# Hybrid layers: the four retention heads' features packed into three tiles, the forget logits moved into spare rows of a rotation tile

## The chip, the cores and the metric

The kernel runs on one core of one Trainium2 chip. The metric is the device time of one launch in microseconds (us); the kernel before was run three times, and the median of the three counts.

## The reference, cut to what matters

The whole program is two blocks of a network on 256 tokens with a model width of 1024, all in float32. The first block (two layers of feed-forward, recurrence and dilated attention) isn't touched by the change. The second block prepends 16 meta tokens (272 tokens in all) and runs two hybrid layers. A hybrid layer multiplies the tokens by one input matrix, splits the product into nine parts, mixes along the tokens in three ways, and multiplies the joined result by one output matrix:

```python
IN_SPLITS = (192, 192, 384, 384, 256, 384, 384, 384, 6)
def hybrid_layer(h, w_in, b_f, ret_gn_g, pool_w, pool_scale, w_out, ...):
    proj = jnp.einsum('bld,de->ble', h, w_in)
    q_r, k_r, v_r, g_r, u_p, q_f, k_f, v_f, f_logit = parts
    o_r = retention_chunkwise(rotary(q_r), rotary(k_r), v_r)
    o_r = silu(g_r) * head_group_norm(o_r, ret_gn_g)
    o_p = multiscale_pool(u_p, pool_w, pool_scale)
    logf = jax.nn.log_sigmoid(f_logit + b_f)
    o_f = forgetting_attention(q_f, k_f, v_f, logf)
    mix = jnp.concatenate([o_r, o_p, o_f], axis=-1)
    mix = jnp.einsum('ble,ed->bld', mix, w_out)
    h = layer_norm_2(ALPHA * h + mix, ln1_g, ln1_b)
```

Retention has 4 heads with 48 features in a query or key and 96 in a value, 384 value features together; `head_group_norm` normalises the 96 features of each head. Forgetting attention has 6 heads of 64 features and one forget logit per head and token. A feed-forward part follows each mixing part.

## The kernel before, in words

**Stages.** `plan()` writes the program as a list of stages, each a multiplication by one weight matrix. A stage is cut into chunks; a chunk holds the weights of one output tile of 128 features and is one DMA of 512 KB or more from SyncE (SP) into one of four slots `raw`. Float32 accuracy comes from a split: ScalarE (ACT) rounds a chunk to `whi` (L1068), VectorE (DVE) subtracts to get `wlo` (L1529), activations are split into `h_hi`/`h_lo` or `x_hi`/`x_lo` the same way, and TensorE (PE) forms three products per 128x128 block (`products`, L511 to L513). One output tile of a stage with K input tiles is thus 3K matmuls. Rounding runs two chunks ahead of PE (`round_ahead` on ACT, `rest_ahead` on DVE).

**A hybrid layer** is the stage `mix` (22 output tiles, K = 8) and the stage `mixo` (8 output tiles, K = `MIX_K` = 9). The order of everything is written out by hand: `MIX_ORDER` lists the output tiles of `mix`, and in `hybrid` of each engine a loop over the step s does the chunk's own work and then what stands under `if s == ...`. An engine's queue runs in program order and waits on semaphores.

The output tiles of `mix` are, in order: `gate 0`, the four rotation tiles `rot` (query halves, then key halves; each head takes 24 of 32 rows, 8 rows are spare), three `vr`, `k 0`, `q 0`, three `v`, `k 1`, `q 1`, `k 2`, `q 2`, two `pool`, and `gate 1` to `gate 3`. There are four gate tiles since each retention head has a tile of its own with 96 of 128 rows in use; rows 96 to 107 of `gate 0` hold the six forget logits twice.

**Around the front of `mix`:** ACT copies each product out of PSUM (`tile`, L1395); behind a norm it also forms `ax` in eight pieces (L1085, two at s = 1, three each at s = 2 and 3). `forget_logits` (ACT L1400 to L1402, with a load of the exp table) follows at s = 2, the copy `sel_r` (L1446) at s = 4. DVE runs `rotate(0)` (L1949 to L1951) at s = 3, the first part of the logarithm of the forget gate (`cumulative_logits(0)`, L1547 and L1548) at s = 4, `rotate(1)` at s = 5. PE runs `ret_scores` (L928) behind tile s = 6; it waits for all four rotations.

**Retention values.** `ret_values(h)` (L892) multiplies the decayed scores of head h by its values: three matmuls (112, 96 and 64 keys; 272, 160 and 64 token columns), 96 output rows, one PSUM bank per head, called for four heads behind tile 10. ACT copies and squares each head (L1438, L1439). `ret_variance` (L944) is four matmuls of 32 output columns each, one per head, side by side in the array. ACT takes the root (L1455), DVE the reciprocal (L2057). `ret_spread(h)` (L952) brings head h's factor to 96 rows, four times, each followed by DVE's `norm_output` (L2007); `gated` (L2015 to L2018) multiplies by the gate and splits, four times.

**Forgetting attention** works in pairs of heads: `fox_scores` (L864, L870), `fox_transposed` (L885), `fox_values` (L907; two heads, each 64 output columns wide, next to each other in the array and in one bank). `mixo` starts with seven of its nine K tiles on the first two chunks (`BEGIN_ORDER`), with `fox_values(2)` between them, and then runs chunk by chunk through `from_h`; DVE adds each output tile (L1645, L1659, L1668) and ACT squares it.

```python
            def ret_values(h):
                pe.wait_ge(vr_centred, l + 1)

                pe.wait_ge(ret_d, RET_HEADS * (l + 1))
                o = ps[0:RET_DV, out_bank[h], :]
                by_values(o, vr_tok, slice(RET_DV * h, RET_DV * (h + 1)), decayed(h)).then_inc(ret_o, 1)
```

Of the kernel before, what the change touches and what calls it, by code (L numbers as in the profile page):

```python
# [18 lines left out]
P = 128  # L19
# [28 lines left out]
RET_HEADS, RET_DK, RET_DV = 4, 48, 96  # L48
HALF_DK = RET_DK // 2
# [3 lines left out]
LOGIT_ROW = RET_DV  # L53
LOGIT_ROWS = 2 * FOX_HEADS
# [16 lines left out]
MIX_K = RET_HEADS + 2 + 3  # L71
MIX_ORDER = ([("gate", 0)] + [("rot", n) for n in range(4)] + [("vr", n) for n in range(3)] + [("k", 0), ("q", 0)]
             + [("v", n) for n in range(3)] + [("k", 1), ("q", 1), ("k", 2), ("q", 2), ("pool", 0), ("pool", 1)]
             + [("gate", n) for n in range(1, 4)])
# [13 lines left out]
C_PS = C_GN + LAYERS_2 * RET_HEADS  # L88
# [6 lines left out]
B_SEL = B_EXP + P  # L95
# [43 lines left out]
def build(nc, x_in, meta_in, par_in, con_in, bias_in, con2_in, poolw_in, weights, out):  # L139
# [34 lines left out]
    ident, ones_d, ones_head = con[:, 0:P], con[:, P:2 * P], con[:, 2 * P:3 * P]  # L174
# [44 lines left out]
    gsb = place("gsb", [RET_HEADS, TOK])  # L219
# [11 lines left out]
    osb = place("osb", [RET_HEADS, TOK])  # L231
# [28 lines left out]
    sqh = place("sqh", [RET_HEADS, TOK])  # L260
# [178 lines left out]
    carry = slice(LOGIT_ROW - HD, LOGIT_ROW - HD + LOGIT_ROWS)  # L439
# [67 lines left out]
    def _(pe):  # L507
# [316 lines left out]
        def hybrid(l):  # L824
# [15 lines left out]
            def fox_scores(pair):  # L840
# [3 lines left out]
                if pair == 0:  # L844
                    pe.wait_ge(c_done, l + 1)
                    pe.wait_ge(sel_done, l + 1)
                    pe.wait_ge(vr_centred, l + 1)

                    pe.wait_ge(ret_sq, RET_HEADS * l + 2)
# [39 lines left out]
            def by_values(o, v, col, weights_t):  # L889

                for k in range(3):
                    last = nc.tensor.matmul(o[:, QT_AT[k]:TOK], v[0:QT[k], k, col],  # L892
                                            weights_t[0:QT[k], KEY_AT[k]:KEY_AT[k] + KEY_COLS[k]], start=k == 0, stop=k == 2)
                return last

            def fox_values(pair):
                heads = (2 * pair, 2 * pair + 1)
                if pair == 0:

                    pe.wait_ge(ret_norm, RET_HEADS * (l + 1))  # L900
# [32 lines left out]
            def ret_values(h):  # L933
                pe.wait_ge(vr_centred, l + 1)

                pe.wait_ge(ret_d, RET_HEADS * (l + 1))
                o = ps[0:RET_DV, out_bank[h], :]
                by_values(o, vr_tok, slice(RET_DV * h, RET_DV * (h + 1)), decayed(h)).then_inc(ret_o, 1)

            def ret_variance():  # L940

                pe.wait_ge(ret_sq, RET_HEADS * (l + 1))
                for h in range(RET_HEADS):
                    ins = nc.tensor.matmul(ps[32 * h:32 * h + 32, 5, 0:TOK], ones_head[0:RET_DV, 0:32], sqh[0:RET_DV, h, :],  # L944
                                           start=True, stop=True, skip_group_check=True)
                ins.then_inc(ret_var, 1)

            def ret_spread(h):
                pe.wait_ge(ret_rstd, l + 1)
                if h:  # L950
                    pe.wait_ge(ret_norm, RET_HEADS * l + h)
                nc.tensor.matmul(ps[0:RET_DV, 5, 0:TOK], con2[32 * h:32 * h + 1, B_EXP:B_EXP + RET_DV],  # L952
                                 std4[32 * h:32 * h + 1, :], start=True, stop=True).then_inc(ret_bc, 1)
# [10 lines left out]
            for s in range(WIN_TILES):  # L964
                tile(s)
                if s == 6:
                    ret_scores()
                if s == 8:
                    pe.wait_ge(acc_free, mix_evicted(st, "vr", 2))
                    pe.wait_ge(ret_d, RET_HEADS * l + 1)  # L970
                    transposes(vr, 3, ((2, 0), (3, 0), (4, 0))).then_inc(vt2_done, 1)
                if s == 10:
                    for h in RET_ORDER:
                        ret_values(h)
                if s == 11:
                    fox_scores(0)
                if s == 12:
                    ret_variance()
                if s == 13:
                    pe.wait_ge(acc_free, mix_evicted(st, "v", 2))  # L980
                    pe.wait_ge(biased, f0 + 1)
                    transposes(vf, 3, ((2, 0), (3, 0), (4, 0))).then_inc(vt2_done, 1)
                if s == 14:
                    ret_spread(0)
                if s == 15:
# [3 lines left out]
                if s == 16:  # L989
                    fox_transposed(1)  # L990
                    ret_spread(2)
                if s == 17:
                    fox_scores(2)
                    ret_spread(3)
                if s == 18:
                    fox_values(0)
                    fox_transposed(2)
                if s == 19:
                    fox_transposed(3)
                if s == 20:  # L1000
                    fox_values(1)
                    fox_transposed(4)
                if s == 21:
# [5 lines left out]
            def ready(k):  # L1009

                if k < RET_HEADS:
                    pe.wait_ge(ret_ready, RET_HEADS * l + k + 1)
                elif k < RET_HEADS + 2:
                    pe.wait_ge(pool_ready, 2 * l + k - RET_HEADS + 1)
                else:
                    pe.wait_ge(at_ready, PAIRS + 3 * l + k - (RET_HEADS + 2) + 1)
# [37 lines left out]
    def _(act):  # L1054
# [314 lines left out]
        def hybrid(l):  # L1369
            st = by_name[f"mix{l}"]  # L1370
            f0 = FOX_HEADS * l
            lr = slice(LOGIT_ROW, LOGIT_ROW + LOGIT_ROWS)
# [24 lines left out]
            def forget_logits():  # L1397
                act.wait_ge(acc_free, mix_evicted(st, "gate", 0))
                bf = par[lr, C_BF + l:C_BF + l + 1]
                nc.scalar.activation(sgate[lr, 0, :], gsb[lr, 0, :], ACT.Identity, bias=bf).then_inc(fx_done, 1)  # L1400
                link(nc.scalar.activation(sgate[lr, 1, :], gsb[lr, 0, :], ACT.Abs, bias=bf))
# [21 lines left out]
            def round_output(hp):  # L1423
                act.wait_ge(pv_done, HEADS + f0 + 2 * hp + 2)
                nc.scalar.activation(h_hi[:, RET_HEADS + 2 + hp, :], acc(5, TOK), ACT.Copy).then_inc(at_hi, 1)
# [8 lines left out]
            hd = slice(0, RET_DV)  # L1434

            def copy_output(n, h):
                act.wait_ge(ret_o, RET_HEADS * l + n + 1)
                nc.scalar.activation(osb[hd, h, :], ps[hd, out_bank[h], 0:TOK], ACT.Copy).then_inc(ret_osb, 1)  # L1438
                nc.scalar.activation(sqh[hd, h, :], ps[hd, out_bank[h], 0:TOK], ACT.Square).then_inc(ret_sq, 1)  # L1439

            for s in range(WIN_TILES):
                round_ahead(st, s // SLOTS, s % SLOTS)
                if s == 2:
                    forget_logits()
                if s == 4:
                    nc.scalar.activation(sel_r[:, :], con2[:, B_SEL:B_SEL + FOX_HEADS * P], ACT.Copy).then_inc(sel_done, 1)  # L1446
                if s == 11:
                    for n, h in enumerate(RET_ORDER):
                        copy_output(n, h)
                if s == 12:  # L1450

                    nc.scalar.activation(spare[:, :], eps[:, :], ACT.Sqrt)
                if s == 13:
                    act.wait_ge(ret_var, l + 1)
                    nc.scalar.activation(std4[:, :], ps[:, 5, 0:TOK], ACT.Sqrt, bias=eps[:, 0:1]).then_inc(ret_std, 1)  # L1455
                    exps(0)
                if s == 14:
                    exps(1)
                    copy_values()
                if s == 16:  # L1460
                    copy_transposed(0)
                if s == 17:
                    copy_transposed(1)
                    exps(2)
                if s == 18:
                    exps(3)
                if s == 19:
# [3 lines left out]
                if s == 20:  # L1471
                    copy_transposed(3)
                    exps(5)
                if s == 21:
                    copy_transposed(4)
                    round_output(1)
                    act.wait_ge(acc_free, mix_evicted(st, "gate", 2))
                    nc.scalar.activation(gsb[:, 0:3, :], gsb[:, 0:3, :], ACT.Silu).then_inc(silu2, 1)
                tile(s)
            act.wait_ge(acc_free, mix_evicted(st, "gate", 3))  # L1480
            nc.scalar.activation(gsb[:, 3, :], gsb[:, 3, :], ACT.Silu).then_inc(silu2, 1)
            copy_transposed(5)
            act.wait_ge(pool_mm, l + 1)
            for m in range(2):
                nc.scalar.activation(h_hi[:, RET_HEADS + m, :], acc(2 + m, TOK), ACT.Copy,
# [29 lines left out]
    def _(dve):  # L1515
# [364 lines left out]
        def hybrid(l):  # L1880
            st = by_name[f"mix{l}"]
            f0 = FOX_HEADS * l
            lr = slice(LOGIT_ROW, LOGIT_ROW + LOGIT_ROWS)
# [25 lines left out]
            def mask_max(h):  # L1909
# [4 lines left out]
                if h < 2:  # L1914

                    dve.wait_ge(ret_o, RET_HEADS * (l + 1))
# [21 lines left out]
            def rest_of_output(hp):  # L1938
                dve.wait_ge(at_hi, PAIRS + 3 * l + hp + 1)
                k = RET_HEADS + 2 + hp  # L1940
# [46 lines left out]
            hd = slice(0, RET_DV)  # L1987

# [13 lines left out]
            def norm_output(h):  # L2002

                n = RET_HEADS * l + h
                dve.wait_ge(ret_bc, n + 1)
                c = C_GN + n
                V.scalar_tensor_tensor(osb[hd, h, :], osb[hd, h, :], par[hd, c:c + 1], ps[hd, 5, 0:TOK],  # L2007
                                       ALU.mult, ALU.mult).then_inc(ret_norm, 1)

            def gated(h):  # L2010

                n = RET_HEADS * l + h
                dve.wait_ge(ret_norm, n + 1)
                dve.wait_ge(silu2, 2 * l + (2 if h == 3 else 1))
                link(V.tensor_tensor(osb[hd, h, :], osb[hd, h, :], gsb[hd, h, :], ALU.mult))  # L2015
                V.tensor_copy(h_hi[hd, h, :], osb[hd, h, :]).then_inc(ret_hi, 1)
# [266 lines left out]
```

## Time and profile before

| what | value |
|---|---|
| time, median of 3 runs | 1783.62 us (1783.58 to 1785.27) |
| the profiled execution's own time | 1781.78 us |
| its span | 1780.0 us |
| PE busy | 1740.9 us, 98% of the span |
| DVE busy | 1249.9 us, 70% |
| ACT busy | 978.6 us, 55% |
| mean share of the DMA queue of the weights | 50.9% of 16 engines |
| first hybrid layer: `mix`, `mixo` | from about 1105 to 1202 us, and to 1232 us |
| second hybrid layer: `mix`, `mixo` | from about 1448 to 1546 us, and to 1575 us |

The span is the time between the first and the last instruction of the profiled execution; its own time is 1.8 us longer, and the median of the runs 1.8 us longer again. Busy shares are means over stages. A float32 matmul stands in the trace as two records, its two passes; a matmul of rounded operands as one. The end of a matmul is modelled, so distances are taken from start to start.

### The profile page before, as it was taken

The numbers are of one execution on the slowest core, as the hardware profiler recorded it, in microseconds if no ns is written. First come the engines' busy times: TensorE is split into PE (matmuls) and PEld (weight loads), VectorE is DVE, ScalarE is ACT, GpSimd is POOL, SyncE is SP. The second block draws the span as 40 slices with busy tenths as digits, with TensorE's granted clock in tenths as the row PEclk, the third lists the DMA queues.
The fourth block names the chain that finished last, engine by engine and source line by source line (L and its number), as shares of the span: only waits on it lengthen the run. The fifth ranks groups of instructions, "written<-read, shape, count | busy, mean of one in ns | idle before, by whom it ended". The sixth has DMA issues, their size and how long they took to land.

```text
span 1780.0 us, 33368 instructions
## 1 busy us (share of the span) xinstructions
PE 1740.9 (98%) x11792; PEld 1578.4 (89%) x11792; DVE 1249.9 (70%) x2186; ACT 978.6 (55%) x1708; POOL 0.2 (0%) x4
## 2 busy tenths in 40 slices
PE   9999998999999999999899999999999999999998
PEld 7888998888899888888788888889999998888887
DVE  6776788777664776677777766768556567787765
ACT  5564595655455555466565544564434364565543
POOL 0000000000000000000000000000000000000000
PEclk9999999999999999999999999999999999999999
DMA  6665365456545656433456652433556534346662
GB/s 223 188 206 195 119 198 172 143 188 205 187 139 167 193 187 214 148 119 121 155 170 187 206 186 79 132 117 120 167 175 200 170 106 129 114 135 196 187 203 87
DMA packets 76637, 290.77 MB, mean 163 GB/s; under 512 B 9344, under 2 KB 11648, under 8 KB 76544
## 3 DMA queue, kind: packets, MB, share of 16 engines
q1 hardware_dynamic: 76544, 289.50, 50.9%
q8 instruction: 62, 1.02, 0.2%
q14 instruction: 31, 0.25, 0.0%
HBM read 288.42 MB, written 1.05 MB: 163 GB/s over the span
## 4 chain that ended last, share of the span: by engine, by line
PE 91%; DVE 5%; ACT 3%; issue 1%; DMA 0%; SPq 0%; ACTq 0%; DVEq 0%
PE psum L519 33%; PE psum L520 17%; PE psum L511 12%; PE psum L513 11%; PE psum L512 11%; PE psum L651 1%; PE psum L762 1%; DVE r_sq L1693 1%; DVE wlo L1529 1%; PE psum L646 1%; PE psum L885 1%; ACT whi L1068 1%; PE psum L892 1%; DVE r_sq L1725 0%; PE psum L864 0%
## 5 line engine op out<-in xcount | busy, mean ns | idle before, releaser
L1529 DVE TENSOR_TENSOR wlo<-raw,whi 128x1024 fp32r<-128x1024 f32 (+3 forms) x496 | 645.2, 1309 | 288.1 <-ACT whi L1068 287.2
L519 PE MATMUL psum<-x_split,whi 128*128 128x512 f32 x1760 | 618.5, 395 | 5.2 <-DVE x_split L1564 2.9
L1068 ACT ACTIVATE whi<-raw 128x1024 fp32r<-128x1024 f32 (+3 forms) x496 | 548.7, 1119 | 40.0 <-PE psum L513 21.2
L520 PE MATMUL psum<-x_split,wlo 128*128 128x256 f32 x1760 | 494.6, 281 | 0.0
L519 PEld LDWEIGHTS psum<-x_split,whi 128*128 128x128 f32 x1760 | 331.5, 188 | 83.3 <-issue 2.9
L511 PE MATMUL psum<-x_split,whi 128*128 128x272 f32 (+1 forms) x1184 | 346.5, 293 | 5.5 <-DVE x_split L1730 5.5
L513 PE MATMUL psum<-x_split,wlo 128*128 128x272 f32 (+1 forms) x1184 | 338.3, 286 | 0.0
L512 PE MATMUL psum<-x_split,whi 128*128 128x272 f32 (+1 forms) x1184 | 337.5, 285 | 0.0
L520 PEld LDWEIGHTS psum<-x_split,wlo 128*128 128x128 f32 x1760 | 331.7, 188 | 0.0
L519 PE MATMUL psum<-h_split,whi 128*128 128x512 f32 x770 | 272.1, 397 | 0.0
L511 PEld LDWEIGHTS psum<-x_split,whi 128*128 128x128 f32 x1184 | 223.0, 188 | 16.2 <-issue 9.8
L512 PEld LDWEIGHTS psum<-x_split,whi 128*128 128x128 f32 x1184 | 223.2, 189 | 0.0
L513 PEld LDWEIGHTS psum<-x_split,wlo 128*128 128x128 f32 x1184 | 223.2, 189 | 0.0
L520 PE MATMUL psum<-h_split,wlo 128*128 128x256 f32 x770 | 216.1, 281 | 0.0
L1136 ACT ACTIVATE small<-psum 128x256 f32<-128x256 f32 x220 | 84.3, 383 | 223.5 <-PE psum L520 223.4
L511 PE MATMUL psum<-h_split,whi 128*128 128x256 f32 (+3 forms) x614 | 177.1, 289 | 9.2 <-DVE h_split L1862 3.8
L519 PEld LDWEIGHTS psum<-h_split,whi 128*128 128x128 f32 x770 | 144.6, 188 | 34.2
L513 PE MATMUL psum<-h_split,wlo 128*128 128x256 f32 (+3 forms) x614 | 174.5, 284 | 0.0
L512 PE MATMUL psum<-h_split,whi 128*128 128x256 f32 (+3 forms) x614 | 174.2, 284 | 0.0
L1171 ACT ACTIVATE r_sq<-r_sq 128x256 f32<-128x256 f32 (+2 forms) x70 | 29.4, 420 | 222.4 <-DVE r_sq L1668 222.4
L520 PEld LDWEIGHTS psum<-h_split,wlo 128*128 128x128 f32 x770 | 145.6, 189 | 0.1
L1603 DVE TENSOR_TENSOR whole<-psum,small 128x256 f32<-128x256 f32 x220 | 93.1, 423 | 62.6 <-ACT small L1136 62.6
(227 smaller groups left out, 1669.9 us busy)
## 6 DMA issues: line engine op xcount, KB each, us to landing
raw<-w_in SPq DMA_DIRECT2D x264, 512.0 KB, 3.6
raw<-w_out SPq DMA_DIRECT2D x96, 704.0 KB, 4.2
raw<-w_mix SPq DMA_DIRECT2D x44, 512.0 KB, 3.6
raw<-w_rg SPq DMA_DIRECT2D x25, 512.0 KB, 3.9
raw<-w_q SPq DMA_DIRECT2D x24, 512.0 KB, 3.6
raw<-w_mixo SPq DMA_DIRECT2D x16, 576.0 KB, 3.7
raw<-w_kv SPq DMA_DIRECT2D x16, 512.0 KB, 3.5
raw<-w_rg_out SPq DMA_DIRECT2D x8, 640.0 KB, 4.0
```

Source lines behind the costliest of these rows:

```text
L511: nc.tensor.matmul(acc(bank, T), whi[slot][0:rows, w], hi, start=start, stop=False)
L512: nc.tensor.matmul(acc(bank, T), whi[slot][0:rows, w], lo, start=False, stop=False)
L513: return nc.tensor.matmul(acc(bank, T), wlo[slot][0:rows, w], hi, start=False, stop=stop)
L519: nc.tensor.matmul(ps[:, bank, :], whi[slot][:, w], split, start=start, stop=False)
L520: return nc.tensor.matmul(part(bank, 0), wlo[slot][:, w], split[:, 0], start=False, stop=stop)
L646: return nc.tensor.matmul(acc(mean_bank(name), T), ones_d, tile[:, t], start=first, stop=last)
L651: ins = nc.tensor.matmul(ps[:, 5, col + m:col + m + 1], tile[:, c:c + P], ones_d[:, 0:1], start=not started, stop=last and m == len(starts ...
L1068: nc.scalar.activation(whi[slot][:, 0:cols], raw[slot][:, 0:cols], ACT.Copy).then_inc(w_hi_done, count)
L1136: nc.scalar.activation(small[:, b, j % 2, :], part(j, 1), ACT.Copy).then_inc(small_out, 1)
L1171: nc.scalar.activation(sq[:, i + j, t], r[:, i + j, t], ACT.Square).then_inc(sq_done, 1)
L1529: V.tensor_tensor(wlo[slot][:, 0:cols], raw[slot][:, 0:cols], f(whi[slot][:, 0:cols]), ALU.subtract).then_inc(w_lo_done, 1)
L1603: ins = V.tensor_tensor(whole[:, b, j % 2, :], part(j, 0), small[:, b, j % 2, :], ALU.add)
```

## The change

`RET_TILES = 3` takes the place of the four tiles of the retention heads. The 384 value features lie one behind the other in three tiles of 128, for the gate, the retention output, its squares and the input tiles of `mixo`; there are three gate tiles, `mix` has 21 chunks and `MIX_K` is 8. The forget logits stand in rows 24 to 29 and 56 to 61 of `rot 0`, so the first tile of `mix` is `rot 0`, and their elementwise work covers rows 0 to 63. Every `if s == ...` is one step earlier. `ret_values` works by tiles, in eight pieces of 64 or 32 output columns; `ret_variance` accumulates three matmuls of four columns; `ret_spread` has three calls with four rows in and 128 columns out.

```diff
-MIX_K = RET_HEADS + 2 + 3
-MIX_ORDER = ([("gate", 0)] + [("rot", n) for n in range(4)] + ...
-             + [("gate", n) for n in range(1, 4)])
+MIX_K = RET_TILES + 2 + 3
+MIX_ORDER = ([("rot", n) for n in range(4)] + ...
+             + [("gate", n) for n in range(RET_TILES)])
-BEGIN_ORDER = (6, 7, 0, 1, 2, 4, 5)
-RET_ORDER = (2, 3, 0, 1)
+BEGIN_ORDER = (5, 6, 0, 1, 3, 4)
+RET_PIECES = tuple((f // P, f % P, n, f // RET_DV) for f, n in
+                   ((0, 64), (64, 32), (96, 32), (128, 64), (192, 64), (256, 32), (288, 32), (320, 64)))
+RET_BANK = (6, 7, 4)
...
-            rows = RET_DV if st.name.startswith("mixo") and k < RET_HEADS else P
-            return products(at(st, i, j)[1], k, h_hi[0:rows, k, t], h_lo[0:rows, k, t], j, T, start, stop, rows)
+            return products(at(st, i, j)[1], k, h_hi[:, k, t], h_lo[:, k, t], j, T, start, stop)
...
+            def ret_values(t):
+                if t == 0:
+                    pe.wait_ge(vr_centred, l + 1)
+                    pe.wait_ge(ret_d, RET_HEADS * (l + 1))
+                for k in range(3):
+                    for tile_, row, n, h in RET_PIECES:
+                        if tile_ != t:
+                            continue
+                        ins = nc.tensor.matmul(ps[row:row + n, RET_BANK[t], QT_AT[k]:TOK],
+                                               vr_tok[0:QT[k], k, P * t + row:P * t + row + n],
+                                               decayed(h)[0:QT[k], KEY_AT[k]:KEY_AT[k] + KEY_COLS[k]],
+                                               start=k == 0, stop=k == 2, skip_group_check=True)
+                ins.then_inc(ret_o, 1)
             def ret_variance():
-                for h in range(RET_HEADS):
-                    ins = nc.tensor.matmul(ps[32 * h:32 * h + 32, 5, 0:TOK], ones_head[0:RET_DV, 0:32], sqh[0:RET_DV, h, :],
-                                           start=True, stop=True, skip_group_check=True)
+                for t in range(RET_TILES):
+                    ins = nc.tensor.matmul(ps[0:RET_HEADS, 5, 0:TOK], of_head[:, RET_HEADS * t:RET_HEADS * (t + 1)], sqh[:, t, :],
+                                           start=t == 0, stop=t == RET_TILES - 1)
-            def ret_spread(h):
-                nc.tensor.matmul(ps[0:RET_DV, 5, 0:TOK], con2[32 * h:32 * h + 1, B_EXP:B_EXP + RET_DV],
-                                 std4[32 * h:32 * h + 1, :], start=True, stop=True).then_inc(ret_bc, 1)
+            def ret_spread(t):
+                nc.tensor.matmul(acc(5, TOK), con2[0:RET_HEADS, B_EXP + P * t:B_EXP + P * (t + 1)], std4[0:RET_HEADS, :],
+                                 start=True, stop=True).then_inc(ret_bc, 1)
...
             for s in range(WIN_TILES):
                 round_ahead(st, s // SLOTS, s % SLOTS)
-                if s == 2:
+                if s == 1:
                     forget_logits()
-                if s == 4:
+                if s == 3:
                     nc.scalar.activation(sel_r[:, :], con2[:, B_SEL:B_SEL + FOX_HEADS * P], ACT.Copy).then_inc(sel_done, 1)
...
-                if s == 2:
-                    V.memset(f(c_parts[:, :]), 0.0)
+                if s == 1:
                     V.memset(den_f[:, :, :], 1.0).then_inc(den_one, 1)
-                if s == 3:
+                if s == 2:
                     rotate(0)
-                if s == 4:
+                if s == 3:
                     cumulative_logits(0)
-                if s == 5:
+                if s == 4:
                     rotate(1)
...
```

ACT's `copy_output`, DVE's `norm_output` and `gated` run three times a layer with 128 rows, not four times with 96. The constants `con2` grow by 256 columns.

## Rows read from the trace of the kernel before

**Rows 1.** The page: busy time of PE, and the chain that ended last.
```profile
PE 1740.9 (98%) x11792; PEld 1578.4 (89%) x11792; DVE 1249.9 (70%) x2186; ACT 978.6 (55%) x1708; POOL 0.2 (0%) x4
...
PE 91%; DVE 5%; ACT 3%; issue 1%; DMA 0%; SPq 0%; ACTq 0%; DVEq 0%
```

**Rows 2.** Busy time by stretch: window, its length, PE, PEld, DVE, ACT, POOL, PEclk, DMA.
```profile
1130.00:1202.00 72.00, 72.00 (x579) 61.51 (x576) 51.81 (x129) 40.30 (x100) 0.00 (x0) 1.00 0.38 121
...
1473.30:1476.70 3.40, 3.40 (x47) 2.66 (x40) 3.20 (x7) 0.00 (x0) 0.00 (x0) 0.50 0.50 148
```

**Rows 3.** Timeline of PE, first layer: start, duration, instruction, wait ahead of it.
```profile
1129.74 2.12 PE L928 MATMUL psum<-rot 32*112 32x272 f32 x48 [2.29 <-DVE rot L1951]
```

**Rows 4.** Timeline of ACT, the front of the first layer's mix.
```profile
1115.06 0.38 ACT L1395 ACTIVATE rot_in<-psum 128x272 f32<-128x272 f32 x1
...
1116.70 0.52 ACT L1400 ACTIVATE sgate<-gsb,par 12x272 f32<-12x272 f32 x1
...
1119.39 0.40 ACT L1395 ACTIVATE rot_in<-psum 128x272 f32<-128x272 f32 x1
...
1121.07 0.38 ACT L1395 ACTIVATE rot_in<-psum 128x272 f32<-128x272 f32 x1
1121.35 1.05 ACT L1068 ACTIVATE whi<-raw 128x1024 fp32r<-128x1024 f32 x1
...
1123.03 0.38 ACT L1395 ACTIVATE rot_in<-psum 128x272 f32<-128x272 f32 x1
...
1124.46 0.40 ACT L1395 ACTIVATE vr<-psum 128x272 f32<-128x272 f32 x1
...
1127.48 0.40 ACT L1395 ACTIVATE vr<-psum 128x272 f32<-128x272 f32 x1 [1.68 <-PE psum L513]
```

**Rows 5.** Timeline of DVE, the same front.
```profile
1119.82 0.44 DVE L1949 TENSOR_TENSOR rtmp<-rot_in,con 128x272 f32<-128x272 f32 x1 [3.93 <-ACT rot_in L1395]
...
1123.76 0.30 DVE L1547 TENSOR_SCALAR prod<-sgate 12x272 f32<-12x272 f32 x1
...
1125.97 1.23 DVE L1529 TENSOR_TENSOR wlo<-raw,whi 128x1024 fp32r<-128x1024 f32 x1
1127.12 0.44 DVE L1949 TENSOR_TENSOR rtmp<-rot_in,con 128x272 f32<-128x272 f32 x1
```

**Rows 6.** Timeline of PE: the retention values of the first layer.
```profile
1144.98 2.41 PE L892 MATMUL psum<-pT_fox,vr_tok 112*96 112x272 f32 x12
...
1149.75 0.39 PE L511 MATMUL psum<-x_split,whi 128*128 128x272 f32 x1
```

**Rows 7.** Timeline of PE: the values of the first pair of attention heads.
```profile
1186.40 1.21 PE L907 MATMUL psum<-pT_fox,vf_tok 112*64 112x272 f32 x12
1187.54 0.59 PE L885 MATMUL psum<-con,s_fox 112*112 112x112 f32 x3
...
1186.91 0.44 PE L907 MATMUL psum<-pT_fox,vf_tok 96*64 96x160 f32 x4
...
1187.05 0.30 PE L907 MATMUL psum<-pT_fox,vf_tok 96*64 96x160 f32 x2
...
1187.28 0.27 PE L907 MATMUL psum<-pT_fox,vf_tok 64*64 64x64 f32 x2
```

**Rows 8.** Timeline of PE: the variance, and the last spread.
```profile
1158.02 0.67 PE L944 MATMUL psum<-sqh,con 96*32 96x272 f32 x8
1158.61 0.39 PE L511 MATMUL psum<-x_split,whi 128*128 128x272 f32 x1
...
1182.56 0.69 PE L952 MATMUL psum<-std,con 1*96 1x272 f32 x2
1183.18 0.39 PE L511 MATMUL psum<-x_split,whi 128*128 128x272 f32 x1
```

**Rows 9.** Timeline of DVE: output tiles of the second layer's mixo.
```profile
1565.58 0.42 DVE L1668 SCALAR_TENSOR_TENSOR r_sq<-psum,ax 128x256 f32<-128x256 f32 x1 [0.34 <-PE psum L513]
...
1568.76 0.42 DVE L1668 SCALAR_TENSOR_TENSOR r_sq<-psum,ax 128x256 f32<-128x256 f32 x1 [0.43 <-PE psum L513]
```

More of the change, by code:

```diff
@@ L52 @@
 FOX_HEADS, FOX_W = 6, 384
-LOGIT_ROW = RET_DV
-LOGIT_ROWS = 2 * FOX_HEADS
+LOGIT_ROW = HALF_DK
+LOGIT_LO = 32 + HALF_DK
 LAYERS_2 = 2
@@ L218, in build @@
     poolw = place("poolw", [LAYERS_2, 2, P])
-    gsb = place("gsb", [RET_HEADS, TOK])
+    gsb = place("gsb", [RET_TILES, TOK])
     qf = place("qf", [3, TOK])
@@ L230, in build @@
     cursor[0] = sq_at
-    osb = place("osb", [RET_HEADS, TOK])
+    osb = place("osb", [RET_TILES, TOK])
     vf_at = cursor[0]
@@ L259, in build @@
     cursor[0] = rot_at
-    sqh = place("sqh", [RET_HEADS, TOK])
+    sqh = place("sqh", [RET_TILES, TOK])
     cursor[0] = rot_in_at
@@ L887, in fox_transposed @@
                 last.then_inc(pT_done, 1)
[L889 to L894, printed above, removed]
             def fox_values(pair):
@@ L971, in hybrid @@
                     transposes(vr, 3, ((2, 0), (3, 0), (4, 0))).then_inc(vt2_done, 1)
+                if s == 9:
+                    for t in range(RET_TILES):
+                        ret_values(t)
                 if s == 10:
-                    for h in RET_ORDER:
-                        ret_values(h)
+                    fox_scores(0)
                 if s == 11:
-                    fox_scores(0)
+                    ret_variance()
                 if s == 12:
-                    ret_variance()
-                if s == 13:
                     pe.wait_ge(acc_free, mix_evicted(st, "v", 2))
@@ L2079, in hybrid @@
                     pool(0)
-                if s == 20:
+                if s == 19:
                     normalise(4)
                     pool(1)
-                if s == 21:
+                if s == 20:
                     normalise(5)
                     rest_of_output(1)
-            for h in range(RET_HEADS - 1):
-                gated(h)
+            for t in range(RET_TILES - 1):
+                gated(t)
             for m in range(2):
                 rest_of_pool(m)
-            gated(RET_HEADS - 1)
+            gated(RET_TILES - 1)
             rest_of_chunk(*ahead(by_name[f"mixo{l}"], 0, 0))
@@ L2128, in constants @@
     con[:, 1] = 1.0 / D
-    con[:RET_DV, 2] = 1.0 / RET_DV
+    feature = np.arange(RET_TILES * P)
+    for h in range(RET_HEADS):
+        mine = (feature // RET_DV == h).reshape(RET_TILES, P)
+        for t in range(RET_TILES):
+            con[mine[t], 2, RET_HEADS * t + h] = 1.0 / RET_DV
     far = -1e33
@@ L2196, in halves @@
         return t.reshape(D, 2 * P)
-    def padded(a):
-        t = np.zeros((D, RET_HEADS, P), w.dtype)
-        t[..., :RET_DV] = a.reshape(D, RET_HEADS, RET_DV)
-        return t
-    g = padded(g)
-    g[:, 0, LOGIT_ROW:LOGIT_ROW + LOGIT_ROWS] = np.tile(logits, 2)
-    rot = np.concatenate([halves(q), halves(k)], axis=1)
-    columns = {"gate": g.reshape(D, RET_HEADS * P), "rot": rot, "vr": v, "pool": u, "q": qf, "k": kf, "v": vf}
+    first = halves(q)
+    for row in (LOGIT_ROW, LOGIT_LO):
+        first[:, row:row + FOX_HEADS] = logits
+    rot = np.concatenate([first, halves(k)], axis=1)
+    columns = {"gate": g, "rot": rot, "vr": v, "pool": u, "q": qf, "k": kf, "v": vf}
     return np.concatenate([columns[kind][:, P * n:P * (n + 1)] for kind, n in MIX_ORDER], axis=1)
-def hybrid_rows(w):
-    t = np.zeros((RET_HEADS, P, D), w.dtype)
-    t[:, :RET_DV] = w[:RET_HEADS * RET_DV].reshape(RET_HEADS, RET_DV, D)
-    return np.concatenate([t.reshape(-1, D), w[RET_HEADS * RET_DV:]], axis=0)
 def tiles(v):
@@ L2259 @@
     par[:, C_LAM:C_GN] = tiles(a["rg_lam"][0])
-    par[:RET_DV, C_GN:C_PS] = a["ret_gn_g_2"].reshape(-1, RET_DV).T
+    par[:, C_GN:C_PS] = tiles(a["ret_gn_g_2"].reshape(-1))
     par[:, C_PS:C_BF] = tiles(a["pool_scale_2"].reshape(-1))
-    par[LOGIT_ROW:LOGIT_ROW + LOGIT_ROWS, C_BF:C_QS] = np.tile(a["b_f_2"].T, (2, 1))
+    for row in (LOGIT_ROW, LOGIT_LO):
+        par[row:row + FOX_HEADS, C_BF:C_QS] = a["b_f_2"].T
     poolw = np.zeros((P, LAYERS_2, 2, P), f32)
```

188 lines of the change are left out of this document (89 added, 99 removed).

## The prediction

> **What bounds the kernel now.** I read the page first: PE is busy for 98% of the span and holds 91% of the chain that ended last [rows 1]. The reader is to see that PE's own work is the time, nearly everywhere, so a matmul taken out is worth its distance to the next one. Then the busy time by stretch: from the retention scores to the end of `mix`, PE is busy for 72.00 of 72.00 us while DVE has 51.81 and ACT 40.30 [rows 2]. Then PE's timeline: the one hole in a hybrid layer's `mix` is the 2.29 us in front of `ret_scores`, where PE waits for DVE's last rotation [rows 3]. Behind that hole PE sets the end; in front of it ACT and DVE do, and there a removed tile is worth only what it takes off their chain. Last I read that chain [rows 4, 5] and the small groups of matmuls that the change rewrites [rows 6 to 8].
>
> **The front: gate 0 and its chunk go.** A tile of `mix` is 24 matmuls; ACT's copies behind two neighbouring tiles start at 1124.46 and 1127.48, so it is 3.02 us of PE, 0.126 a matmul [rows 4]. PE would reach `ret_scores` 3.02 us earlier, at 1124.4 (now the hole begins at 1129.74 - 2.29 = 1127.45 [rows 3]). What it waits for moves as follows. `forget_logits` now comes in front of the copy of `rot 1`, behind only two `ax` pieces, so it starts where the copy of `rot 0` stood, at 1115.06, not 1116.70; from its start to the copy of `rot 1` are 1119.39 - 1116.70 = 2.69 us, so that copy starts at 1117.75 [rows 4]. `rotate(0)` follows 0.43 us behind it (1119.82 - 1119.39), at 1118.18 [rows 4, 5]. ACT then has three `ax` pieces and the copy of `rot 2` (1.68 us from copy to copy), three more `ax` pieces, `sel_r` and the copy of `rot 3`. Before, copy 1 to copy 3 took 3.64 us with one rounding of 1.05 us (overlapping a little) inside; the second three pieces, some 1.3 us, take its place, so copy 3 starts at about 1117.75 + 4.0 = 1121.8, the rounding of chunk 6 at 1122.1, and its remainder on DVE at 1123.2. DVE had `rotate(0)` and the first logarithm part done by then: 1118.18 + 2.6, and 2.21 us (1123.76 to 1125.97), give 1123.0 [rows 5]. The remainder takes 1.15 us and `rotate(1)` 2.62 (1127.12 to 1129.74 [rows 3, 5]): PE starts `ret_scores` at 1127.0. Gain 2.7 us a layer, and the hole is 2.6 us, no shorter than before. The bounds are 1.23 us (only the chunk's remainder [rows 5] leaves a chain that DVE sets) and 3.02. The cleared `c_parts` (a memset) lay in DVE's idle time of 3.93 us [rows 5] and counts for nothing. The chunk's DMA is issued by SP and prefetched; PE and DVE wait for no landing there.
>
> **Retention values.** Now 1149.75 - 1144.98 = 4.77 us for four heads [rows 6]. After it there are 24 matmuls, not 12, of 64 or 32 columns. Two pieces of equal width share the array: the attention heads' pair, with the same keys and token columns, takes 1187.54 - 1186.40 = 1.14 us for both [rows 7]. The variance has four of 32 columns at once, eight passes in 0.59 us [rows 8]. Tile 1 (64 + 64) is therefore 1.14 us. Tiles 0 and 2 mix one piece of 64 with two of 32, which no row shows together. A row shows what a change of shape costs: the passes with 96 keys follow each other at 0.14 us (1186.91, 1187.05), and the first pass with 64 keys comes 0.23 us later, 1187.28, after both heads of the old shape, 0.09 more than the work [rows 7]. So I take it that different widths don't overlap: a mixed tile is two rounds, one of the wide piece and one of the two narrow ones, and a round by itself costs 0.59 us with 272 columns [rows 8], 0.37 with 160 (1186.91 to 1187.28) and 0.26 with 64 (1187.28 to 1187.54) [rows 7], 1.22 together. The sum is 1.14 + 4 x 1.22 = 6.02 us, 1.25 more than now. The bounds: all pieces of a tile at once, 3 x 1.14 = 3.42, a gain of 1.35; every piece alone, 8 x 1.22 = 9.76, a loss of 4.99. I take 6.02, the value nearest to the row on a change of shape.
>
> The Trainium skill, "TensorEngine Tiling (Array Packing)", Key Properties, says that different tiles run in parallel but that a change of the tiling mode, not merely of the tile, drains the array. By that rule the two widths here, 64 and 32, are two modes and the sum is the 6.02 above; without it the sum would be the 3.42 of the lower bound. The trace agrees with it where the keys change, at 0.09 us a change [rows 7]; for two column widths in one tile no row shows it.
>
> **Variance and spread.** The variance was one round, 0.59 us [rows 8]; now it is three matmuls that accumulate in the same rows and can't lie side by side, six passes. A pass of 272 columns is 0.23 us (0.62 / 2 less the change of shape of 0.09 [rows 7, 8]). Four more passes are 0.91 us. Bounds: nothing, and 4 x 0.31 = 1.24. One spread of 0.62 us goes (1182.56 to 1183.18 [rows 8]).
>
> **The output stage.** K falls from 9 to 8, 24 matmuls fewer a layer over eight output tiles. With 272 tokens that is 24 x 0.126 = 3.02 us [rows 4]; in the second layer, with 256 tokens, an output tile of 27 is 3.18 us, 0.118 a matmul, and 24 are 2.83 [rows 9]. DVE idles 0.34 to 0.43 us a tile there [rows 9] and its remainder gets 128 columns shorter, 0.14 us at the rate of rows 5, while a tile of PE gets 0.35 shorter, so 0.15 us or more is left: PE still sets the pace. That a K tile's rows are 128 now, not 96, changes no column count, and I cost it at nothing.
>
> **What costs nothing.** ACT's copies and squares, `norm_output` and `gated`, one fewer each a layer, lie beside 72 us of gapless PE [rows 2]; were they to surface they would be a gain. More rows per elementwise instruction cost nothing: with 272 elements a row, 12 rows take 0.30 to 0.52 us and 128 rows 0.38 to 0.44 [rows 4, 5]. Moving every step by one keeps each wait's distance to the steps around it, so no new wait appears behind the scores; values that end 1.25 us later only add slack. The 256 more columns of `con2` are 0.13 MB in SP's queue under the feed-forward part, where the queue is half idle.
>
> **The sum.** A layer's `mix`: -2.70 + 1.25 + 0.91 - 0.62 = -1.16; two of them -2.32. `mixo`: -3.02 - 2.83 = -5.85. Together -8.2 us. Against the profiled execution's 1781.78 that is 1773.6; the median of the runs is 1.8 us above it, so **1775.4**. What a measurement of this kernel can tell from no change is 0.2%, 3.6 us.
>
> **The clock.** In the second layer the granted clock was 0.50 (1.2 of 2.4 GHz) from 1473.3 to 1476.7 us [rows 2], right behind the same hole of 2.29 us that left it at full in the first. At half clock 3.4 us do the work of 1.7. With holes of 2.6 us this may vanish or come in both layers: 1.7 us either way, kept for the range.
>
> **Rivals.**
> - *All pieces of a tile at once.* For it: the variance runs four widths of 32 together [rows 8], and nothing in the array's rows forbids 64 beside 32. Against: the 0.09 us of a change of shape [rows 7]. Values 3.42 us, 2.6 less a layer: -13.4, 1770.2. Chance 0.24.
> - *The front gives back its tile.* ACT or DVE doesn't come earlier than by one remainder, 1.23 us, as the logarithm or the table load now stands ahead of the rotation; the hole grows to 4.1 us. Against: ACT's row of `forget_logits` has nothing in front but `ax` pieces [rows 4]. 1.47 less a layer: -5.2, 1778.4. Chance 0.12.
> - *Every piece alone.* 3.74 more a layer: -0.7, 1782.9, no change that can be told. Against: rows 7 and 8 show neighbours overlapping. Chance 0.09.
> - *Slower: the passes of the pieces alternate between widths,* each drained, at the 0.31 us of half a spread [rows 8] whatever its columns: 48 passes, 14.9 us a layer in `ret_values`, 8.9 more than I take. +9.6 us, 1793.2. It decides against the change by more than 0.2% from 11.9 us for the values of a layer. For it: two passes of neighbours do interleave. Against: no row has short passes at that price in a row. Chance 0.05.
> - That the change doesn't do what it says I exclude: chunk counts and K are fixed by the diff.
>
> **Numbers.** The forecast has 0.50. Its own range is 1772.5 to 1778.5 (clock, variance, front). The range over the cases runs from the first rival less the clock's 1.7, 1768.5, to 1780.5 over the second; it leaves out the third and the slower one, and some of the tails. Faster by over 0.2%: forecast, first and second rival, 0.86 less little, 0.85. Same: the third, 0.10. Slower: 0.05.
>
> **What would show it.** In the profile after: 21 copies at L1395's line a layer, `rot 1`'s copy some 2.7 us behind `forget_logits`, `ret_scores` 9.2 us behind that copy (1127.0 - 1117.75; before 1129.74 - 1119.39 = 10.35), with a hole of some 2.6 us ahead of it; the values' group 6.0 us from its first matmul to the next tile, and the starts of pieces of 64 and of 32 apart, not 0.01 us from each other (that would be the first rival); the variance 1.5 us; output tiles of `mixo` at 3.0 and 2.83 us. The prediction is wrong if a hole opens behind the scores, if the values take under 4 or over 9 us, or if DVE sets the pace of `mixo`.

## The result, and the profile after

The changed kernel takes 1773.35 us (median of 4 runs, 1772.47 to 1777.25), the one before 1783.6 us beside it: a ratio of 0.9949, 95% interval 0.9936 to 0.9961, 9.1 us less by the ratio. A second set of runs (e8 below) gave 0.9946, 0.9933 to 0.9960. The profiled execution has a span of 1771.8 us, 8.2 less than before. The page of the kernel after, busy time:

```profile
PE 1734.6 (98%) x11736; PEld 1567.5 (88%) x11736; DVE 1241.3 (70%) x2174; ACT 972.9 (55%) x1700; POOL 0.2 (0%) x4
...
PE 91%; DVE 5%; ACT 2%; issue 1%; DMA 0%; SPq 0%; ACTq 0%; DVEq 0%
```

PE is still the bound, as in [rows 1]. Busy time by stretch, kernel after; the first line answers to the first of [rows 2], the second is a stretch of the second layer, and the third lies behind the first layer's `mixo`:

```profile
1129.00:1201.00 72.00, 72.00 (x552) 59.51 (x551) 49.33 (x126) 39.70 (x98) 0.00 (x0) 1.00 0.35 117
1466.50:1469.90 3.40, 3.40 (x43) 2.90 (x36) 3.23 (x8) 0.00 (x0) 0.00 (x0) 0.50 0.50 159
1231.00:1234.40 3.40, 3.40 (x18) 3.40 (x18) 2.25 (x6) 1.56 (x4) 0.00 (x0) 0.50 0.30 114
```

From the scores to the end of `mix` PE is again busy without a gap, and the second layer's scores again stand at half clock. The third line is a stretch of half clock behind the first layer's `mixo`, where the kernel before has full clock. The timeline of PE after, from the first layer; the groups answer to [rows 3, 6, 8]: the scores, then of the values the two passes of tile 0's wide piece, its two narrow pieces, the first records of tiles 1 and 2 and the tile of `mix` behind them, then the variance and one spread.

```profile
1126.29 2.12 PE L926 MATMUL psum<-rot 32*112 32x272 f32 x48 [2.20 <-DVE rot L1955]
...
1141.62 0.44 PE L941 MATMUL psum<-s_fox,vr_tok 112*64 112x272 f32 x1
1141.90 0.39 PE L941 MATMUL psum<-s_fox,vr_tok 112*64 112x272 f32 x1
1142.22 0.42 PE L941 MATMUL psum<-s_fox,vr_tok 112*32 112x272 f32 x2
...
1144.11 0.44 PE L941 MATMUL psum<-pT_fox,vr_tok 112*64 112x272 f32 x1
...
1145.25 0.42 PE L941 MATMUL psum<-pT_fox,vr_tok 112*32 112x272 f32 x2
...
1147.73 0.40 PE L517 MATMUL psum<-x_split,whi 128*128 128x272 f32 x1
...
1156.01 1.54 PE L951 MATMUL psum<-sqh,con 128*4 128x272 f32 x6
1157.48 0.39 PE L517 MATMUL psum<-x_split,whi 128*128 128x272 f32 x1
...
1171.08 0.72 PE L959 MATMUL psum<-std,con 4*128 4x272 f32 x2
1171.73 0.40 PE L517 MATMUL psum<-x_split,whi 128*128 128x272 f32 x1
```

From start to start: values 1147.73 - 1141.62 = 6.11 us (4.77 before), variance 1.47 (0.59), a spread 0.65 (0.62), the hole 2.20 (2.29). The values by tiles: tile 0 takes 1144.11 - 1141.62 = 2.49 us, tile 1 (64 and 64 columns) 1.14, tile 2 takes 2.48. In the mixed tile 0 the narrow pieces start 0.60 us behind the wide one, when both its passes have started. ACT's front after, answering to [rows 4]:

```profile
1114.73 0.51 ACT L1406 ACTIVATE sgate<-rot_in,par 64x272 f32<-64x272 f32 x1
...
1117.30 0.38 ACT L1401 ACTIVATE rot_in<-psum 128x272 f32<-128x272 f32 x1
...
1118.82 0.38 ACT L1401 ACTIVATE rot_in<-psum 128x272 f32<-128x272 f32 x1
1119.09 1.34 ACT L1091 ACTIVATE ax<-r_sq,ab 128x272 f32<-128x272 f32 x3
1120.33 0.84 ACT L1450 ACTIVATE sel_r<-con 128x768 fp32r<-128x768 f32 x1
1121.07 0.38 ACT L1401 ACTIVATE rot_in<-psum 128x272 f32<-128x272 f32 x1
1121.34 1.06 ACT L1074 ACTIVATE whi<-raw 128x1024 fp32r<-128x1024 f32 x1
```

DVE's front after, answering to [rows 5]; and DVE in the second layer's `mixo`, answering to [rows 9]:

```profile
1120.65 1.84 DVE L1552 RECIPROCAL prod<-prod 64x272 f32<-64x272 f32 x1
1122.53 1.22 DVE L1533 TENSOR_TENSOR wlo<-raw,whi 128x1024 fp32r<-128x1024 f32 x1
1123.67 0.43 DVE L1953 TENSOR_TENSOR rtmp<-rot_in,con 128x272 f32<-128x272 f32 x1
...
1563.91 0.42 DVE L1672 SCALAR_TENSOR_TENSOR r_sq<-psum,ax 128x256 f32<-128x256 f32 x1 [0.21 <-PE psum L519]
...
1566.74 0.42 DVE L1672 SCALAR_TENSOR_TENSOR r_sq<-psum,ax 128x256 f32<-128x256 f32 x1 [0.21 <-PE psum L519]
```

An output tile of `mixo` is 2.83 us and DVE waits 0.21 us for it: PE still sets the pace, and DVE has less time to spare than before.

**Where the time went.** From PE's starts in both traces, first layer, from the first product of `mix` to the norm: front 24.03 to 20.89 (-3.15), values +1.35, variance +0.87, spreads 4 x 0.62 to 3 x 0.65 (-0.54), `mixo` 29.06 to 26.09 (-2.97), and 0.09 more between the tile ahead of the values and their first piece (0.22 us from record to record; before, with a matmul of 96 columns behind that tile, 0.13). Sum -4.35; the whole stretch went from 126.25 to 121.91. Second layer: front -3.12, values +1.35, variance +0.87, spreads -0.54, `mixo` 27.54 to 24.77 (-2.77), small rest +0.04: -4.17. Together -8.5 us of a span that fell by 8.2; the rest of the program, which the change leaves as it was, is 0.35 us longer in this profile.

### The profile page after: what moved, and what is told of

It is laid out like the page before. It is cut to its first block, busy times and chain, and to the rows that moved or that the text cites. A ratio compares the mean times of both kernels' runs of the same rounds, so it can differ in the third digit from the quotient of the medians.

```text
span 1771.8 us, 33209 instructions
## 1 busy us (share of the span) xinstructions
PE 1734.6 (98%) x11736; PEld 1567.5 (88%) x11736; DVE 1241.3 (70%) x2174; ACT 972.9 (55%) x1700; POOL 0.2 (0%) x4
## 4 chain that ended last, share of the span: by engine, by line
PE 91%; DVE 5%; ACT 2%; issue 1%; DMA 0%; SPq 0%; ACTq 0%; DVEq 0%
PE psum L525 33%; PE psum L526 17%; PE psum L517 12%; PE psum L519 11%; PE psum L518 11%; PE psum L656 1%; PE psum L767 1%; DVE r_sq L1697 1%; PE psum L651 1%; DVE wlo L1533 1%; PE psum L941 1%; PE psum L890 1%; DVE r_sq L1729 1%; ACT whi L1074 0%; PE psum L869 0%
## 5 line engine op out<-in xcount | busy, mean ns | idle before, releaser
L1533 DVE TENSOR_TENSOR wlo<-raw,whi 128x1024 fp32r<-128x1024 f32 (+2 forms) x494 | 640.8, 1305 | 291.0 <-ACT whi L1074 289.5
L1074 ACT ACTIVATE whi<-raw 128x1024 fp32r<-128x1024 f32 (+2 forms) x494 | 544.9, 1116 | 38.2 <-PE psum L519 20.0
L517 PE MATMUL psum<-x_split,whi 128*128 128x272 f32 (+1 forms) x1168 | 342.2, 293 | 4.9 <-DVE x_split L1734 4.9
L519 PE MATMUL psum<-x_split,wlo 128*128 128x272 f32 (+1 forms) x1168 | 333.8, 286 | 0.0
L518 PE MATMUL psum<-x_split,whi 128*128 128x272 f32 (+1 forms) x1168 | 332.8, 285 | 0.0
L517 PEld LDWEIGHTS psum<-x_split,whi 128*128 128x128 f32 x1168 | 220.2, 189 | 14.9 <-issue 8.5
L517 PE MATMUL psum<-h_split,whi 128*128 128x256 f32 (+1 forms) x598 | 172.6, 289 | 9.3 <-DVE h_split L1866 3.8
L519 PE MATMUL psum<-h_split,wlo 128*128 128x256 f32 (+1 forms) x598 | 170.0, 284 | 0.0
L518 PE MATMUL psum<-h_split,whi 128*128 128x256 f32 (+1 forms) x598 | 169.7, 284 | 0.0
```

The source lines that it names most:

```text
L517: nc.tensor.matmul(acc(bank, T), whi[slot][0:rows, w], hi, start=start, stop=False)
L518: nc.tensor.matmul(acc(bank, T), whi[slot][0:rows, w], lo, start=False, stop=False)
L519: return nc.tensor.matmul(acc(bank, T), wlo[slot][0:rows, w], hi, start=False, stop=stop)
L1074: nc.scalar.activation(whi[slot][:, 0:cols], raw[slot][:, 0:cols], ACT.Copy).then_inc(w_hi_done, count)
L1533: V.tensor_tensor(wlo[slot][:, 0:cols], raw[slot][:, 0:cols], f(whi[slot][:, 0:cols]), ALU.subtract).then_inc(w_lo_done, 1)
```

## The experiments

Each kernel is the changed one with the edit shown.

**e1, the same 24 matmuls in rounds of one width.** What the mixed tiles cost is the one term with far bounds.

```diff
+RET_ROUNDS = (tuple(p for p in RET_PIECES if p[0] == 1), tuple(p for p in RET_PIECES if p[0] != 1 and p[2] == 64),
+              tuple(p for p in RET_PIECES if p[2] == 32))
+RET_ORDER = (1, 0, 2)
-                    for tile_, row, n, h in RET_PIECES:
-                        if tile_ != t:
-                            continue
+                    for tile_, row, n, h in RET_ROUNDS[t]:
...
-                ins.then_inc(ret_o, 1)
+                        if k == 2 and (tile_, row) in ((1, 64), (0, 96), (2, 32)):
+                            ins.then_inc(ret_o, 1)
...
```

Bank and rows of each output stay what they were; ACT copies the tiles in the order 1, 0, 2.

> The changed kernel with its 24 matmuls of retention values in another order: first the two 64-column pieces of tile 1, then the two of tiles 0 and 2 side by side, then all four 32-column pieces together. Same matmuls, no mixing of widths. Theory (different widths don't overlap, equal widths do, so rounds count): three rounds, 3.45 us a layer from the first matmul to the next tile instead of 6.11, the time 5.3 us less than the changed kernel's, ratio to before about 0.992. Rival (each piece has a price of its own, whatever stands beside it): still 6.1 us, ratio 0.995.

Measured: 1769.0 us, ratio 0.9920 (0.9903 to 0.9936). The values take 3.41 us a layer in both layers. PE's timeline of e1, the starts of the three rounds and the next tile:

```profile
1143.97 0.44 PE L942 MATMUL psum<-s_fox,vr_tok 112*64 112x272 f32 x1
1143.98 0.44 PE L942 MATMUL psum<-pT_fox,vr_tok 112*64 112x272 f32 x1
...
1145.12 0.44 PE L942 MATMUL psum<-s_fox,vr_tok 112*64 112x272 f32 x1
1145.12 0.44 PE L942 MATMUL psum<-pT_fox,vr_tok 112*64 112x272 f32 x1
...
1146.26 0.42 PE L942 MATMUL psum<-s_fox,vr_tok 112*32 112x272 f32 x2
1146.27 0.42 PE L942 MATMUL psum<-pT_fox,vr_tok 112*32 112x272 f32 x2
...
1147.38 0.40 PE L520 MATMUL psum<-x_split,whi 128*128 128x272 f32 x1
```

The reader is to see pairs that start within 0.01 us, and 1.12 to 1.15 us a round. Pieces of tiles 0 and 2, in different banks, and four narrow pieces run together; the piece has no price of its own. The rival is out. The gain in the runs, 1773.35 or 1772.11 (e8) to 1769.0, is 3.1 to 4.4 us, short of the 5.3 expected. In the profile the values give 2 x 2.70 = 5.4 us, and 1.56 are lost again: this profile has a stretch of half clock at the scores of both layers, the changed kernel's only in the second, and in the first layer the values begin 16.89 us behind the start of the scores, not 15.33. Whether that explains the other runs isn't shown.

**e2, all pieces 32 columns wide.**

```diff
-                   ((0, 64), (64, 32), (96, 32), (128, 64), (192, 64), (256, 32), (288, 32), (320, 64)))
+                   ((f, 32) for f in range(0, RET_TILES * P, 32)))
```

> The changed kernel with every 64-column piece cut into two of 32: 12 pieces and 36 matmuls, all of one width, four side by side per tile, tiles still one after the other. Theory (rounds count, not matmuls): 3.45 us a layer like the packed rounds, 5.3 us less than the changed kernel. Rival (the number of matmuls or pieces sets the price): 6.11 x 36 / 24 = 9.2 us a layer, 6 us more than the changed kernel.

Measured: 1769.81 us, ratio 0.9927 (0.9910 to 0.9944); values 3.35 us a layer, with half as many matmuls again. The runs are 3.5 us below the changed kernel's 1773.35, short of the 5.3 expected; in the profile the two layers' `mix` and `mixo` are 5.4 us shorter, and the rest of the program is 0.3 longer. PE's timeline of e2, first record and next tile:

```profile
1142.40 0.44 PE L941 MATMUL psum<-s_fox,vr_tok 112*32 112x272 f32 x4
...
1145.75 0.39 PE L517 MATMUL psum<-x_split,whi 128*128 128x272 f32 x1
```

36 matmuls in 3.35 us against 24 in 6.11: the number of matmuls sets nothing here, and what made the values long is the mixing of widths.

**e3, the variance's three matmuls in column groups of their own.**

```diff
-                    ins = nc.tensor.matmul(ps[0:RET_HEADS, 5, 0:TOK], of_head[:, RET_HEADS * t:RET_HEADS * (t + 1)], sqh[:, t, :],
-                                           start=t == 0, stop=t == RET_TILES - 1)
+                    ins = nc.tensor.matmul(ps[32 * t:32 * t + RET_HEADS, 5, 0:TOK], of_head[:, RET_HEADS * t:RET_HEADS * (t + 1)],
+                                           sqh[:, t, :], start=True, stop=True, skip_group_check=True)
```

> The changed kernel with the three matmuls of the variance in three column groups of the array, not accumulated; it leaves out the sum of the partial variances over the tiles. Theory (accumulation in the same rows keeps them from lying side by side): 0.60 us a layer, as before the change, instead of 1.47, and everything behind 0.87 us a layer earlier. Rival (more rows, or the load of four columns, made it longer): between 0.9 and 1.5 us.

Measured, a single run (1771.93 us): PE's timeline of e3, the variance and the tile behind it.

```profile
1156.43 0.63 PE L951 MATMUL psum<-sqh,con 128*4 128x272 f32 x6
1156.99 0.39 PE L517 MATMUL psum<-x_split,whi 128*128 128x272 f32 x1
```

0.56 us with 128 rows and four columns: neither makes it longer. What does is that all three write the same rows of the output; whether the accumulation or the shared columns of the array is to blame, no run here separates.

**e4, the forget logits a step later on ACT.**

```diff
-                if s == 1:
+                if s == 2:
                     forget_logits()
```

> The changed kernel with the forget logits of ACT one step later (s = 2), so that the copy of rot 1 comes 2.6 us earlier and DVE can start the first rotation that much earlier. Theory (ACT's own chain to the rounding of chunk 6 sets the hole, whatever the order within it): the scores start within 0.15 us of the changed kernel's against the stage's first matmul (20.89 us), the hole stays 2.1 to 2.2 us. Rival (the copy of rot 1 and the first rotation set it): the scores 1.3 to 2.2 us earlier.

Measured, a single run (1771.37 us): the scores 20.88 us behind the stage's first matmul (20.91 in e8), the hole 2.18. DVE's timeline of e4:

```profile
1112.82 0.43 DVE L1953 TENSOR_TENSOR rtmp<-rot_in,con 128x272 f32<-128x272 f32 x1
...
1116.97 1.85 DVE L1552 RECIPROCAL prod<-prod 64x272 f32<-64x272 f32 x1
1120.13 1.23 DVE L1533 TENSOR_TENSOR wlo<-raw,whi 128x1024 fp32r<-128x1024 f32 x1 [1.31 <-ACT whi L1074]
```

DVE's first rotation came 2.5 us earlier in the stage than in e8 (9.79 us behind its first matmul, not 12.33), and DVE then idled 1.31 us for ACT's rounding of chunk 6. The first rotation is not what the hole hangs on.

**e5, and `sel_r` out of ACT's chain.** The edit of e4, and:

```diff
-                if s == 3:
+                if s == 6:
                     nc.scalar.activation(sel_r[:, :], con2[:, B_SEL:B_SEL + FOX_HEADS * P], ACT.Copy).then_inc(sel_done, 1)
```

> The changed kernel with the forget logits at s = 2 and ACT's copy sel_r moved from s = 3 to s = 6, behind the rounding of chunk 6. Theory (ACT's chain up to the rounding of chunk 6 sets the hole in front of the scores): sel_r's 0.75 us leave the chain, the scores start at 20.15 us of the stage instead of 20.89, the hole is 1.45 us. Rival (by now DVE's rotations and the logarithm set it): no more than 0.1 us earlier than with the logits alone.

Measured, a single run (1769.09 us): scores at 20.09 us in the first layer and 20.78 in the second (21.54 in e8). PE's timeline of e5:

```profile
1124.45 0.94 PE L926 MATMUL psum<-rot 32*112 32x272 f32 x9 [1.45 <-DVE rot L1955]
```

The hole lost the 0.75 us of `sel_r`, in both layers, as the theory on ACT's chain has it.

**e6, and the last rotation ahead of the chunk's remainder on DVE.** The edits of e5, and:

```diff
             for s in range(WIN_TILES):
+                if s == 4:
+                    rotate(1)
                 rest(s)
...
-                if s == 4:
-                    rotate(1)
```

> As e5, and DVE does rotate(1) ahead of the remainder of chunk 6, which PE needs only behind the scores. Theory (the hole is DVE's order, not its load): the hole in front of the scores goes altogether, 2.2 us a layer, 4.4 us less than the changed kernel or up to 0.3 less of a gain, as the centred values then come only just in time; ratio to before about 0.9925. Rival (DVE is behind by as much, and the wait comes back in front of the retention values): PE idles 1.5 to 2.2 us there instead, and the time stays at the changed kernel's.

Measured: 1767.19 us, ratio 0.9917 (0.9901 to 0.9932), 4.9 us less than e8 on the same chip. Scores at 18.48 us in the first layer and 19.27 in the second, 2.4 and 2.3 earlier than in e8; the values follow 15.33 us behind them, as in e8, so no wait came back. PE's timeline of e6:

```profile
1124.33 0.29 PE L519 MATMUL psum<-x_split,wlo 128*128 128x272 f32 x1
1124.54 2.12 PE L926 MATMUL psum<-rot 32*112 32x272 f32 x48
```

The hole was the order of two chains, not load: of its 2.2 us, 0.75 went with ACT's order (e5) and the rest with DVE's. It was in the kernel before too, and the change kept it.

**e7, e6 with the rounds of e1.**

> e6 and the packed rounds of e1 together. Theory (both gains lie on PE's chain and add up): 4.3 + 5.3 = 9.6 us less than the changed kernel, some 1764, ratio to before 0.989. Rival (with PE 4.9 us earlier in a layer DVE's sums of the logits come too late, and the attention scores wait): PE idles up to 1 us a layer in front of fox_scores, and the gain is 7.5 to 8.5 us.

Measured: 1762.81 us (1761.69 to 1763.43), ratio 0.9892 (0.9877 to 0.9908), 9.3 us less than e8 and the fastest of all. Busy time by stretch of e7, from the first product of `mix` to shortly ahead of the norm, both layers:

```profile
1106.00:1222.00 116.00, 116.00 (x949) 103.97 (x948) 90.19 (x198) 69.14 (x150) 0.00 (x0) 1.00 0.37 123
1440.00:1556.00 116.00, 115.64 (x954) 103.23 (x953) 91.33 (x201) 70.08 (x152) 0.00 (x0) 1.00 0.37 123
```

In the first layer PE has no idle time left. The 0.36 us of the second lie at the start of the stage, where PE waits for DVE's `x_split`; the attention scores never wait for DVE. The rival's wait is out, and the gains add up: between the profiles of e6 and e7 the two layers differ by 5.4 us, twice the 2.70 of the values.

**e8, the changed kernel again.** No edit.

> The changed kernel again, beside the others on the same chip, for a narrower interval. Theory: ratio to before 0.9950, and in the profile values of 6.11 us a layer and a hole of 2.2 us in both. Stretches of half clock may fall elsewhere than in the first profile, each worth up to 1.7 us of span.

Measured: 1772.11 us (1771.67 to 1772.84), ratio 0.9946 (0.9933 to 0.9960). Values 6.11 us, hole 2.20 in both layers; the stretches of half clock fall at other times than in the first profile, and the span is 1769.9, not 1771.8.

**e9, a ninth K tile on PE alone.**

```diff
                 last = h_products(st, i, j, k, len(todo) == tiles and n == 0, n == len(todo) - 1)
+                if st.name.startswith("mixo") and k == 2:
+                    h_products(st, i, j, k, False, False)
```

> The changed kernel with K back at nine in the output stages as far as PE is concerned: each of the eight output tiles of mixo multiplies the third retention tile a second time (it is counted twice in the sum), 24 matmuls more a layer, no DMA and no rounding more. Theory (PE sets the pace of mixo and a K tile is worth its 24 matmuls): from the first products of mixo to the norm 3.0 us more in the first layer and 2.8 in the second, ratio to before 0.998. Rival (DVE or the weights set the pace since K is eight, so part of the eighth saved tile was never gained): less than 2 us a layer more.

Measured: 1779.63 us, ratio 0.9983 (0.9973 to 0.9992). `mixo` to the norm: 28.91 us in the first layer against 26.11 in e8, 2.80 more; 27.27 against 24.78 in the second, 2.49 more. DVE's timeline of e9, output tiles of the first layer:

```profile
1223.64 0.44 DVE L1674 SCALAR_TENSOR_TENSOR r_sq<-psum,ax 128x272 f32<-128x272 f32 x1 [0.69 <-PE psum L519]
1227.02 0.44 DVE L1674 SCALAR_TENSOR_TENSOR r_sq<-psum,ax 128x272 f32<-128x272 f32 x1 [0.69 <-PE psum L519]
```

A tile is 3.38 us again and DVE waits for PE. So the K tile saved was won nearly whole; the missing 0.2 to 0.3 us a layer against 3.0 and 2.8 stay unexplained (PE has no gap there in either). The runs are 7.5 us above e8's where the two stages give 5.3; of the rest, the profile of e9 has 2.3 us ahead of the first `mix`, where the two kernels are the same.

## Why the prediction was right

The forecast was -8.2 us and 1775.4; measured were 1773.35 and, in e8, 1772.11, -9.1 and -9.6 by the ratios, with intervals that hold 8.2. Its mechanisms held, step by step; that the total is so near is partly luck, since the front gave more than was taken and the values less. By its steps:

- **Front, -2.70 a layer taken; -3.15 and -3.12 measured.** The mechanism held (e4, e5: ACT's chain to the rounding of chunk 6). The term was too small: the logits took 2.57 us to the copy of `rot 1`, not 2.69, and from that copy to the copy of `rot 3` it was 3.77 us (1117.30 to 1121.07), not 4.0. The forecast had DVE ready 0.2 us ahead of ACT (1123.0 against 1123.2); the two came out as good as equal: DVE's reciprocal ended at 1122.49, ACT's rounding at 1122.40, and the remainder started at 1122.53. That the scores didn't move in e4, where DVE's part was done early, shows that ACT's chain alone would have held them. The hole was forecast at 2.6 us and is 2.20. It even shrank by 0.09, and that took the gain past the 3.02 that the forecast gave as the upper bound: the bound assumed that the hole can't get shorter.
- **Values, +1.25 taken; +1.35 measured.** 6.11 us against 6.02: 2.49, 1.14 and 2.48 for the tiles, where the forecast had 2.44, 1.14 and 2.44. The step from the 0.09 us of a change of shape [rows 7] to "widths don't overlap" was right: e1 and e2 take the mixing away and get 3.41 and 3.35 us, the 3.42 of the first rival, which the change as written doesn't reach. The Trainium skill, "TensorEngine Tiling (Array Packing)", Key Properties, says that a change of the tiling mode drains the array and a mere change of tile doesn't. The trace agrees: pieces of one width start within 0.01 us of each other (e1), and the wide and narrow pieces of a tile never did.
- **Variance +0.91, measured +0.87** (0.62 / 2 less 0.09 is 0.22 a pass, not 0.23, and four are 0.88); **spread -0.62, measured -0.54,** as each of the three left takes 0.65 with 128 columns, not 0.62. The forecast priced the one removed and forgot that the others change.
- **`mixo` -3.02 and -2.83, measured -2.97 and -2.77.** PE kept the pace with 0.21 us of DVE's idle time left a tile (the forecast's 0.15 or more is 0.13 to 0.22 by its own numbers); e9 shows it from the other side.
- **Costed at nothing:** no wait opened behind the scores (72.00 of 72.00 us).
- **The clock:** at the scores it neither vanished nor doubled in the profile of the change; it stayed in the second layer. Elsewhere the stretches of half clock moved (one more at 1231.0 us, and at 893 us one of 3.4 us in place of 6.8), and up to the end of the second `mixo` both profiles have 23.9 us of them.
- **Rivals.** All pieces at once (3.42 us), each alone (9.76) and alternating passes (14.9): out by the 6.11 us. The front that gives its tile back: out by 3.15.

The sum by steps is -8.5 us where the forecast had -8.2. The medians of the runs differ by 9.7 to 10.3. The two profiles of the changed kernel show where such a difference can come from: e8's span is 1.9 us shorter than the first one's, yet its two layers' `mix` and `mixo` take as long (244.7 against 244.6 us). The difference lies ahead of the first `mix`, which begins at 1103.18 us in e8 and at 1105.40 in the first profile; over all eleven profiles it begins between 1103.0 and 1106.2, though up to there the kernels differ at most by the longer load of `con2`. So a term of 2 us can't be read from two medians, and what makes this part longer or shorter stays open.

## What to carry to other kernels

The matmuls of 64 and 32 columns here cost rounds, not pieces: put together those of equal width in different column groups, across tiles and banks if need be, and don't alternate widths, which here cost 2.7 us a layer for no work. Before a matmul tile is counted as saved, see whether what PE waits for behind it gets earlier too; and where PE waits for one step of an engine, see whether that step can pass work that isn't due yet.

## What was not expected

The half clock goes with the hole. In all eight profiles of the changed kernel's variants and of the kernel before in which PE waits 2.2 to 2.3 us ahead of the scores (before, the change, e1 to e4, e8, e9), a stretch of 3.4 us at 0.50 (1.2 GHz) stands at the second layer's scores; in e1 and e3 the first layer has one too. In e5, e6 and e7, where the hole is 1.45 us or gone, neither layer has one there. Two of them in e1, busy time by stretch:

```profile
1127.60:1131.00 3.40, 3.40 (x46) 2.60 (x39) 3.23 (x7) 0.00 (x0) 0.00 (x0) 0.50 0.44 151
1465.50:1468.90 3.40, 3.40 (x45) 2.77 (x38) 3.23 (x7) 0.00 (x0) 0.00 (x0) 0.50 0.51 153
```

In the profiles closing the hole was thus worth more than its length: the scores of the second layer took 3.22 us in e8 and 2.05 in e6 and e7, and from their start to the values it was 16.87 us in e8 and 15.33 in e6, 1.54 less. The runs can't show this apart: e6 is 4.9 us faster than e8, the earlier scores alone are 4.7, and its profile has a stretch of half clock at 1437.7 us, ahead of the second `mix`, that e8's hasn't. Stretches of half clock also stand at places without this hole, so it is one occasion of several. Why the second layer meets it always and the first only in two of eight stays open.
